# Stick-breaking attention, key index, sparse attention and merge as one run of work on one core: no barriers between them, tails moved beside the next stage, gates first

## The reference, cut to what matters

```python
def mixer(h, pos, w_in, w_a, w_b, w_o):
    proj = h @ w_in
    q_a, k_a, v_a, q_b, k_b, v_b, qi, ki, wi, g_a, g_b = jnp.split(proj, offsets, axis=-1)
    y_a = stick_breaking_attention(q_a, k_a, v_a)          # 8 heads of 128
    y_a = y_a @ w_a
    y_b = dsa_attention(rope(q_b), rope(k_b), v_b, rope(qi), rope(ki), wi)   # 8 heads of 128
    y_b = y_b @ w_b
    merged = jax.nn.sigmoid(g_a) * y_a + jax.nn.sigmoid(g_b) * y_b
    return merged @ w_o

# in dsa_attention, per query: which 64 keys are looked at
dots = einsum('qhi,ki->qhk', qi, ki) * 64 ** -0.5           # 16 index heads of 64
score = einsum('qh,qhk->qk', wi, relu(dots)) * 16 ** -0.5
_, idx = lax.top_k(where(visible, score, -inf), 64)
p = softmax(logits over the chosen keys)
```

## Time and profile before

| what | value |
|---|---|
| median of three runs | 3244.68 us (3238.67 to 3249.91) |
| the profiled execution | 3239.63 us, of which span 3237.9 us |
| PE busy | 2978.7 us, 92% of the span |
| DVE busy | 2055.7 us, 63% |
| ACT busy | 1342.7 us, 41% |
| mean transfer rate | 181 GB/s |
| stretch that the change touches | from the first projection of sb at 123 us to the end of merge at 903 us |

### The profile page before, as it was taken

How to read it: one execution, slowest core, us unless ns; L and a number is a source line. 1 busy time by engine, 2 the same in 40 slices (tenths; PEclk the granted TensorE clock), 3 DMA queues, 4 the chain that set the end, 5 groups by cost and what they waited for, 6 DMA issues and landing times.

```text
span 3237.9 us, 62102 instructions
## 1 busy us (share of the span) xinstructions
PE 2978.7 (92%) x24818; PEld 2836.6 (88%) x24818; DVE 2055.7 (63%) x2868; ACT 1342.7 (41%) x1892; POOL 167.2 (5%) x288
## 2 busy tenths in 40 slices
PE   1698999799999999998999999979699999999998
PEld 1698899799998888887999999978698999998997
DVE  7775878677656666665445555756557666665445
ACT  1354333333335555554444444313345444443443
POOL 0121012122200000000000000012000000000000
PEclk6798999899999999999999999989899999999999
DMA  9776367688854655554555455510153555554552
GB/s 360 264 255 192 105 201 242 207 273 288 269 195 144 198 190 181 194 182 157 184 190 171 153 147 171 165 41 4 53 182 117 182 185 186 185 181 164 187 181 104
DMA packets 407396, 585.37 MB, mean 181 GB/s; under 512 B 20385, under 2 KB 368673, under 8 KB 389857
## 3 DMA queue, kind: packets, MB, share of 16 engines
q1 hardware_dynamic: 384720, 516.24, 47.8%
q0 software_dynamic: 20480, 67.13, 6.1%
q10 hardware_dynamic: 2064, 0.13, 0.0%
HBM read 581.35 MB, written 2.10 MB: 180 GB/s over the span
## 4 chain that ended last, share of the span: by engine, by line
PE 74%; DVE 13%; DMA 6%; issue 3%; ACT 2%; DVEq 0%; PEld 0%; PEldq 0%; POOLq 0%; SPq 0%; POOL 0%; ACTq 0%
PE bank L458 15%; PE bank L459 15%; PE bank L460 15%; PE bank L465 15%; PE bank L466 8%; DMA late_ring<-w_ada_dram 5%; PE bank L1164 3%; DVE wlo L392 3%; DVE work L1987 2%; DVE work L1955 1%; DMA ring<-w_ada_dram 1%; PE bank L735 1%; ACT whi L381 1%; PE bank L1049 0%; DVE mats L2487 0%
## 5 line engine op out<-in xcount | busy, mean ns | idle before, releaser
L392 DVE TENSOR_TENSOR wlo<-ring,whi 128x1024 fp32r<-128x1024 f32 x908 | 1084.0, 1220 | 528.9 <-ACT whi L381 527.1
L381 ACT ACTIVATE whi<-ring 128x1024 fp32r<-128x1024 f32 x908 | 941.6, 1052 | 1046.6 <-PE bank L460 688.4
L458 PE MATMUL bank<-hx,whi 128*128 128x256 f32 (+2 forms) x2704 | 781.3, 289 | 31.0 <-DVE wlo L392 21.5
L460 PE MATMUL bank<-hx,wlo 128*128 128x256 f32 (+2 forms) x2704 | 772.5, 286 | 0.0
L459 PE MATMUL bank<-hx,whi 128*128 128x256 f32 (+2 forms) x2704 | 771.8, 285 | 0.0
L465 PE MATMUL bank<-hx,whi 128*128 128x512 f32 x2112 | 741.1, 394 | 1.6 <-DVE wlo L392 1.1
L466 PE MATMUL bank<-hx,wlo 128*128 128x256 f32 x2112 | 594.7, 282 | 0.0
L458 PE MATMUL bank<-xs,whi 128*128 128x256 f32 (+1 forms) x1920 | 545.3, 284 | 39.0 <-DVE xs L451 38.4
L458 PEld LDWEIGHTS bank<-hx,whi 128*128 128x128 f32 x2704 | 515.6, 191 | 42.6 <-DVE wlo L392 24.2
L460 PE MATMUL bank<-xs,wlo 128*128 128x256 f32 (+1 forms) x1920 | 544.9, 284 | 0.0
L459 PE MATMUL bank<-xs,whi 128*128 128x256 f32 (+1 forms) x1920 | 544.2, 283 | 0.0
(11 more groups left out here) (307 smaller groups left out, 2731.4 us busy)
## 6 DMA issues: line engine op xcount, KB each, us to landing
ring<-w_in_dram SPq DMA_DIRECT2D x136, 1024.0 KB, 5.4
ring<-w_up_dram SPq DMA_DIRECT2D x88, 1024.0 KB, 5.1
ring<-w_down_dram SPq DMA_DIRECT2D x88, 1024.0 KB, 4.8
ring<-w_gate_up_dram SPq DMA_DIRECT2D x88, 1024.0 KB, 5.1
late_ring<-w_ada_dram POOLq DMA_DIRECT2D x256, 256.0 KB, 4.0
ring<-w_ada_dram SPq DMA_DIRECT2D x32, 1024.0 KB, 7.3
ring<-w_o_dram SPq DMA_DIRECT2D x16, 1024.0 KB, 4.8
ring<-w_out_dram SPq DMA_DIRECT2D x16, 1024.0 KB, 5.2
```

The source lines that it names most:

```text
L381: nc.scalar.activation(half_of(whi, u, h, n), ring[:, u % PLAN[phase][3], h * n // 2:(h + 1) * n // 2], ACT.Copy)\
L392: nc.vector.tensor_tensor(half_of(wlo, u, h, n), ring[:, u % PLAN[phase][3], h * n // 2:(h + 1) * n // 2], half_of(whi, u, h, n).bitcast(F ...
L458: nc.tensor.matmul(out_ap, a[0], b[0], start=start, stop=False, **kw)
L460: return nc.tensor.matmul(out_ap, a[1], b[0], start=False, stop=stop, **kw)
```

## The change

What each part does:

1. **Index beside the last heads of sb.** `phase_end(3)` is gone. After the fourth iteration PE makes the scores of the last two heads and block 3's sums, goes on to ki, and makes the cumulative sums after ki and the values after the first pair of qi. ki and wi share bank 0; the four pairs of qi use banks 1, 2, 0, 1.
2. **Dots inside qi and dsa.** The dots of heads 0 to 7 stand between the quarters of the last pair of qi, those of heads 8 to 15 between the quarters of the first projection of dsa. Banks 3 to 7 take them in turn. `keep_warm` is gone, and `phase_end(4)` too.
3. **Choice of keys beside the first iteration of dsa.** DVE adds the scores of the heads and makes the rounds of the search between the rests of dsa's first six units; five of the eight rounds and the mask stand after them, ahead of the second iteration.
4. **Block 4 of `late`** moves from dsa's first iteration to the index stage, four steps after the masks of the last sb heads, then four after each of three pairs of qi.
5. **Merge without a barrier, gates first.** `phase_end(5)` is gone. Each iteration makes the two gates first (banks 0 and 1) and then the two outputs (banks 2 and 4). The turning and the values of the last two dsa heads stand behind the first and the second gate of the first iteration. The outputs are split in two pieces, `yas` and `ybs` (128 x 2048 each); `mergedT` moves to where the heads' buffers were.
6. `w_o`, `w_a` and `w_b` lie in one tensor `w_oab` in memory. `phase_end(6)` counts for four barriers, so later waits keep their numbers.

The diff, cut to its core:

```diff
+            repeat(pe, 4, sb)
+            sb_scores(4)
+            late_sum(3)
             for quarter in range(4):
...
+            sb_sums(4)
+            qi_free = [(k_read, 4), (v_read, 4), (evac["ki"], 2), (evac["qi"], 2)]
+            for s in range(4):
+                pe.wait_ge(*qi_free[s])
+                for quarter in range(4):
...
+                    last.then_inc(used, 1)
+                    if s == 3:
+                        head_dots(2 * quarter)
+                        head_dots(2 * quarter + 1)
+                if s == 0:
+                    sb_values(4)
...
-            pe.wait_ge(relu_done, 9)
-            keep_warm(0, 40)
-            phase_end(pe, 4)
...
+                def dots_between(quarter):
+                    head_dots(2 * quarter + 8)
+                    head_dots(2 * quarter + 9)
+                pe.wait_ge(evac["qi"], 6)
+                project("dsa", 0, i, False, 0, between=dots_between)
...
+            def merge(i):
+                if first(i):
+                    dsa_scores(4)
+                late_sum(i + 7)
+                for s, b in enumerate((GATE_A, GATE_B)):
...
+                    if first(i):
+                        (dsa_turns, dsa_values)[s](4)
+                for s, b in enumerate((OUT_A, OUT_B)):
+                    if first(i):
+                        pe.wait_ge(y_lo, s + 1)
...
```

On DVE, from the end of sb to the second iteration of dsa:

```diff
+            sb_masked(4)
+            late(4, 0, 4)
+            sb_softplus(4)
+            rest_unit("qi", 0, 0)
+            sb_differences(4)
+            rest_unit("qi", 1, 0)
...
+            for s in range(3):
+                rest_unit("qi", 2 * s + 2, 0)
+                rest_unit("qi", 2 * s + 3, 0)
+                rope_pair(s)
+                late(4, 4 * s + 4, 4 * s + 8)
...
+            head_scores(0, 4)
+            rest_unit("dsa", 0, 0)
+            head_scores(4, 8)
+            rope_pair(3)
+            rest_unit("dsa", 1, 0)
+            head_scores(8, 12)
+            rest_unit("dsa", 2, 0)
+            head_scores(12, IDX_HEADS)
+            rest_unit("dsa", 3, 0)
             step(nc.vector.scalar_tensor_tensor(score, seen, UNSEEN / NEG, score, ALU.mult, ALU.add))
+            rest_unit("dsa", 4, 0)
+            top_rounds(0, 1)
+            rest_unit("dsa", 5, 0)
+            top_rounds(1, 3)
+            rest_unit("dsa", 0, 1)
+            multiplied(dve, "dsa", 1, 0)
+            rope(qT[:].rearrange("p a t -> p (a t)"), bank[:, 0, :], 2 * T, tabs128, 64, q2_read, 1)
+            rest_unit("dsa", 1, 1)
+            multiplied(dve, "dsa", 5, 0)
+            nc.vector.tensor_copy(vS[:].rearrange("p a t -> p (a t)"), bank[:, 2, :]).then_inc(v2_read, 1)
+            rope(kT[:].rearrange("p a t -> p (a t)"), bank[:, 1, :], 2 * T, tabs128, 64, k2_read, 1)
+            top_rounds(3, TOPK // 8)
...
```

On DVE, in merge:

```diff
+                for u in range(2, 6):
+                    rest_unit("merge", u, i)
+                    if first(i) and u == 5:
+                        dve.wait_ge(y_hi, 2)
+                        nc.vector.tensor_tensor(ybs[:, :, 1, :], ybT, ybs[:, :, 0, :].bitcast(F32), ALU.subtract).then_inc(y_lo, 1)
+                    late(i + 8, 4 * (u - 2), 4 * (u - 1))
+                for s in range(2):
+                    multiplied(dve, "merge", 4 + s, i)
...
+                    if s == 0:
+                        rest_unit("merge", 0, i + 1) if not last else rest_unit("wo", 0, 0)
...
+                rest_unit("merge", 1, i + 1) if not last else rest_unit("wo", 1, 0)
```

## The result

The changed kernel takes 3174.1 us (median of four runs, 3171.9 to 3174.4) where the kernel before took 3245.1 us in the same comparison: a ratio of 0.978, with a 95% interval from 0.977 to 0.980. That is 71 us faster. The profiled executions differ by 65.5 us (3239.63 and 3174.16 us, spans 3237.9 and 3172.4 us); all that follows is read from these two.

The account below looks back on a forecast made before the run. It took PE's idle time at three barriers and some iteration starts as the bound. Terms 13.1 + 26.7 - 2.8 + 17.4 + 13.6 = 68.0 us gave 3171.6 from the profile or 3176.7 from the median; forecast 3175 us, range 3152 to 3207.

Parts of the forecast that it names:

- A: Behind sb: ki directly follows block 3's sums, the last heads' cumulative sums and values come later; 13.1 us gained.
- B: End of qi to dsa's second iteration: dots and choice of keys go beside PE's products; 26.7 us gained.
- C: dsa's later iterations: DVE sets the pace and PE waits 2 us in the second iteration; 2.8 us lost.
- D: Behind dsa: merge's products start without waiting for the last heads, whose transposes and values move into merge; 17.4 us gained.
- E: Merge: rests one unit ahead and column sums waiting for no sigmoid give 35.1 us per iteration; 13.6 us gained.
- The clock: Slow stretch around ki: 10 us at half clock, 5 us lost, left as it was, so no term in the sum.
- DVE's lag: Between qi and dsa's second iteration: DVE late by about 0.9 us, then some 2.6; 3.5 us taken off the gain.
- Rival 1: From qi to dsa: DVE becomes the bound and its waits hold up rests, 20 us lost, 3195 us; chance 0.18.
- The slow start: Start of merge: clock at half after the wait for block 7, allowed 2.9 us.
- Rival 2: Merge: held by its transfers, not its order, keeping 37 us per iteration, 3189 us; chance 0.12.
- Rival 4: dsa and merge: late loads issued by POOL starved beside a denser DVE, 40 us lost, 3215 us; chance 0.04.
- Rival 3: qi, dots and dsa's first iteration: clock stays low, 90 us more, slower than before at 3265 us; chance 0.02.

Follow-up runs that it names:

- wi144: Changed kernel with ki's narrow index-weight products moving 144 columns instead of 16, wanted columns copied out: 3163.0 us, ratio 0.976 to the kernel before.
- late_early: Changed kernel with eight late steps of block 4 moved from between qi's pairs into DVE's idle time during ki: 3161.3 us, ratio 0.976 to the kernel before.
- peeled: Changed kernel with two half rests of dsa's iteration 1 put between the last search rounds: 3170.6 us, ratio 0.978 to the kernel before.
- outputs_first: Changed kernel with dsa's last heads finished alone ahead of merge and merge's old order restored: 3205.5 us, ratio 0.988 to the kernel before.
- rest_first: Changed kernel with the rests PE needs first in dsa and merge put ahead of late steps: 3169.2 us, ratio 0.977 to the kernel before.
- mixed: Changed kernel with ki's same products reordered, six narrow ones after each three wide: 3174.4 us, ratio 0.979 to the kernel before.

## Why the prediction was right, point by point

The forecast was 3175 us, the median is 3174.1; the terms added up to 68.0 us and the profiled executions differ by 65.5, the medians by 71.0. The steps named were right, each with its mechanism, but that the forecast is good to 1 us is luck. Between block 3's sums and the end of merge, which is all that the terms cover, the gain is 62.5 us and not 68.0: A and B 31.9 (39.8 forecast), C -4.2 (-2.8), D and E 34.7 (31.0). Another 3.0 us lie outside.

**A (16.2 us earlier, 3.1 back; 13.1).** ki began 16.3 us earlier than before relative to block 3's sums (288.77 - 287.86 against 305.71 - 288.48), the cumulative sums and values waited for nothing, and at a full clock the order is worth 14.0 us.

**The clock (left out of the sum).** This is the term that failed. The prediction left the slow stretch in ki "where it is". It named the right cause, shown by wi144, but took its length for a constant of the kernel: 10 us before, 24 in the changed kernel's profile, 10 to 34 in versions with the same narrow products. The 13.7 us that it grew by cost 6.8 us of what A and B gave. Why it grew was not found. The Trainium skill (TensorE: Matmul & The Clock Gate, Part 1) has the gate released by activity, and by that rule the prediction gave 5 us more if the idle time ahead of ki went. The idle time went, and the clock fell all the same, with PE busy for every us of the stretch: the trace does not agree with what I had made of the rule.

**B (26.7 us).** A and B together were to bring dsa's second iteration 39.8 us forward; it came 31.9 earlier (32.6 less the 0.6 that were there before). 6.8 of the missing 7.9 are the clock, 2.2 are DVE's lag, taken at 3.5 us and measured at 1.56 + 1.29 + 2.83 = 5.7; the remainder is 1.1 us better than worked out. Undoing B alone costs 24.9 us at its place. Rival 1 (DVE as the bound, 20 us lost) had the right engine and the wrong size: 2.2 us more than the forecast allowed, and late_early shows that four fifths of the waits go with eight late steps.

**C (-2.8 us).** Iteration 1 takes 46.9 us in place of 43.1, -3.8, and by block 7's sums it is -4.2. (The forecast works out 2.9 us and enters 2.8.) The wait ahead of its second projection, forecast at 2 us, is 2.82, and peeled shows that DVE's pace holds it.

**D (19.8 us less 2.4).** From block 7's sums to merge's first product: 21.7 before, 1.7 after, so 19.9 us.

**E (13.6 us).** Merge with the 2.4 us counted in D was to take 288.3 us and takes 284.8. The order is what did it: merge's waits of 12.1 us in outputs_first (12.2 in the kernel before) are gone. The slow start is near the 2.9 us forecast (the window 552.90:572.00 has a clock of 0.80, 7.6 us at the low level, 3.8 us lost, a part of it in the sums ahead of merge). The 0.4 us allowed for each iteration for late loads were not needed: 35.0 us of products in 35.0. That is 3.5 us better than forecast and cancels half of the clock's miss. Rival 2 (held by transfers) is refuted by outputs_first, and by transfers that now run at 300 to 314 GB/s. Rival 4 (late loads starved) by their median of 4.6 us against 4.4, beside a DVE that has become denser; the rule of the Trainium skill (SBUF — State Buffer, SBUF: two separate sides) that would starve them did not show; the Trainium skill has it for operations of VectorE in a two-port mode, and no run tells whether these are such. Rival 3 (clock stays low through qi and dsa) did not come: 0.97 from 355 to 415 us.

The last 3.0 us of the 65.5 lie outside the change: 0.6 ahead of block 3's sums and 2.4 behind merge. From the product behind merge to the end all versions have the same program, and it took between 2322.6 and 2328.9 us in their profiled executions (2330.3 in the kernel before), so that 2.4 us there are not larger than the spread.

**The range.** Its good end doesn't follow from its parts. The better ends listed are 5 for A and B, 3 for D and 16 - 13.6 = 2.4 for E, together 10.4 us, which gives 3165 and not 3156; the worse ends, 32.6 us, give 3208, where 3206 stands. And qi's last product began at 372.2 in the kernel before, not at 372.6, which makes the 75.1 us of B 75.4. None of this changes which way the forecast fell.

## What to carry to other kernels

Read the granted clock of every stretch, not only of the ones with idle time: a stretch can be busy for all of its length and still run at half speed, and how long it does can vary between executions of the same program, so that a version can look slower or faster by several us for no reason in its order. Where a barrier goes, add up the waiting engine's own work over the stretch behind it and ask which engine sets the pace there: where it was DVE (peeled, rest_first) moving a wait brought nothing or a third of it, and work put into DVE's idle time (late_early) brought four fifths. Gains found one by one in a stretch that one engine paces don't add up.

## What the runs showed of the hardware that was not expected

- Products of 16 moving columns bring the granted clock to 0.50 while PE is busy for 19.70 of 19.70 us, whether they come 24 in a row or six at a time (mixed); with 144 columns in their place the clock is 1.00 from 288.5 to 320 us (wi144). The slow stretch was 10 to 34 us long, 24 to 31 in five executions with the same program up to there.
- At the full clock a product of 16 columns takes as long as one of 144 and nearly as long as one of 256, each with its own weights: they start 0.11, 0.11 and 0.12 us apart (late_early, wi144).
- The transfer engines were busy to 0.93 at 314 GB/s for a whole merge iteration without one wait of PE, and loads of 256 KB issued by POOL landed after 4.6 us in the median (4.4 before).
